# Expert weights of a streaming MoE step: who issues the up blocks

## What is computed

```python
def hier_moe(h, w_r1, b_r1, w_r2, b_r2, w_g, w_u, w_d):
    x = h.reshape(B * S, Dm)
    ...  # routing: top-1 of 4 groups, then top-2 of 8 experts in the group
    for e in range(N_EXPERTS):                 # 32 experts, D_EXPERT = 512
        a = jax.nn.silu(x @ w_g[e]) * (x @ w_u[e])
        y = y + gate[:, e:e + 1] * (a @ w_d[e]).astype(jnp.float32)
    return y.astype(h.dtype).reshape(B, S, Dm)
```

## Time and profile before

| what | us |
|---|---|
| median of three runs | 932.31 |
| the profiled execution | 933.53 |
| its span, first to last instruction | 931.7 |
| PE busy | 776.2 (83%) |
| ACT busy | 116.7 (13%) |
| loads of expert weights, median from issue to landing: down / gate / up | 17.1 / 20.9 / 23.9 |

### The profile page before, as it was taken

One profiled execution on the slowest core, in us unless ns is written; L12 is line 12 of the kernel. 1 busy time (PEld: TensorE's weight loads), 2 busy tenths in 40 slices (PEclk: granted clock), 3 DMA queues, 4 the chain that ended last, 5 costly groups with the idle time before them and its releaser, 6 DMA issues.

```text
span 931.7 us, 11609 instructions
## 1 busy us (share of the span) xinstructions
PE 776.2 (83%) x4652; PEld 463.7 (50%) x4652; DVE 191.4 (21%) x482; ACT 116.7 (13%) x279; POOL 123.9 (13%) x220
## 2 busy tenths in 40 slices
PE   5999999698889999889878797878888788888840
PEld 4756655445654655545544454444545454545420
DVE  2002332225232062411110101010100110101114
ACT  3101311014112042000000000000000000000001
POOL 2100000100001001232111212121111211111123
PEclk9899999989899999789999899999999998999975
DMA  8946952330056434508999999999999999999814
GB/s 247 376 150 225 327 182 91 113 124 1 2 191 253 151 113 160 191 19 340 403 415 422 403 417 414 409 411 387 419 404 421 415 417 416 415 413 418 365 50 129
DMA packets 71599, 261.27 MB, mean 280 GB/s; under 512 B 14055, under 2 KB 30463, under 8 KB 62960
## 3 DMA queue, kind: packets, MB, share of 16 engines
q1 hardware_dynamic: 63232, 244.57, 67.3%
q0 software_dynamic: 8192, 16.27, 5.2%
q10 hardware_dynamic: 144, 0.00, 0.0%
HBM read 249.37 MB, written 24.97 MB: 294 GB/s over the span
## 4 chain that ended last, share of the span: by engine, by line
PE 53%; DMA 34%; DVE 5%; issue 3%; ACT 1%; POOL 1%; SPq 1%; ACTq 0%; POOLq 0%; DVEq 0%
DMA ring<-in_w_exp_gate 32%; PE pA L1048 12%; PE pA L1054 10%; PE pA L1448 10%; PE pS L1468 7%; PE pTr L1041 1%; DMA zone<-y_d,slot 1%; PE pS L1125 1%; PE pS L1104 1%; DVE zone L1853 1%; PE pA L1356 1%; PE pA L1201 1%; PE pA L1071 1%; PE pS L1118 1%; PE pS L1456 1%
## 5 line engine op out<-in xcount | busy, mean ns | idle before, releaser
L1448 PE MATMUL pA<-ring,zone 128*64 128x256 f32 x1984 | 256.3, 417 | 53.4 <-DMA ring<-in_w_exp_gate 53.4
L1448 PEld LDWEIGHTS pA<-ring,zone 128*64 128x64 f32 x1984 | 160.9, 151 | 146.9 <-DMA ring<-in_w_exp_gate 57.2
L1468 PE MATMUL pS<-ring,zone 128*64 128x512 f32 x512 | 117.0, 598 | 21.6 <-DVE zone L1853 21.6
L1048 PE MATMUL pA<-hT,ring 128*128 128x320 f32 x320 | 92.5, 449 | 2.3 <-DVE hT L1541 2.0
L1468 PEld LDWEIGHTS pS<-ring,zone 128*64 128x64 f32 x512 | 37.2, 137 | 80.8 <-issue 77.8
L1048 PEld LDWEIGHTS pA<-hT,ring 128*128 128x128 f32 x320 | 62.4, 198 | 28.0 <-issue 3.1
L968 ACT ACTIVATE zone<-pS 128x512 f32<-128x512 f32 x32 | 19.1, 597 | 370.8 <-PE pS L1468 370.8
L1842 DVE TENSOR_TENSOR zone<-zone,pA 128x256 f32<-128x256 f32 x32 | 13.5, 422 | 252.0 <-ACT zone L961 252.0
L697 POOL COPY idx_cur<-srow 64x1 uint32 (+1 forms) x32 | 5.7, 178 | 336.3 <-PE pTr L1433 334.8
L1853 DVE COPY zone<-pS 128x256 f32<-128x256 f32 x32 | 13.6, 425 | 178.9 <-PE pS L1456 178.9
L1054 PE MATMUL pA<-ring,hT 128*128 128x512 f32 (+1 forms) x112 | 49.9, 604 | 0.0
(11 more groups left out here) (265 smaller groups left out, 648.1 us busy)
## 6 DMA issues: line engine op xcount, KB each, us to landing
ring<-in_w_exp_down SPq DMA_DIRECT2D x32, 2048.0 KB, 17.1
ring<-in_w_exp_up SPq DMA_DIRECT2D x31, 2048.0 KB, 23.9
ring<-in_w_exp_gate SPq DMA_DIRECT2D x31, 2048.0 KB, 20.9
ring<-in_w_in SPq DMA_DIRECT2D x6, 2048.0 KB, 14.3
y_d<-zeros SPq DMA_DIRECT2D x1, 8192.0 KB, 43.7
ring<-in_w_out SPq DMA_DIRECT2D x2, 2048.0 KB, 9.4
ring<-in_w_ck SPq DMA_DIRECT2D x1, 2048.0 KB, 17.2
ring<-in_w_cv SPq DMA_DIRECT2D x1, 2048.0 KB, 21.2
```

What stands on the lines that cost most here:

```text
L1048: last = mm(bank[:, 0:n], w[:, c, m * P:(m + 1) * P], xT[:, c, 0:n], start=c == 0, stop=c == C - 1)
L1448: last = mm(pA[b][half * SLOTS:(half + 1) * SLOTS, x * HF:(x + 1) * HF], xeT[:, b, c, :], w[:, c, half * HF:(half + 1) * HF], start=c == 0 ...
L1468: last = mm(pS[b][half * SLOTS:(half + 1) * SLOTS, 0:512], aT[:, b, f % 2, (f // 2) * SLOTS:(f // 2 + 1) * SLOTS], w[:, f, half * 512:(hal ...
```

## The change

The up blocks of experts 3 to 31 (29 loads) are no longer issued by SP but by ACT, on ACT's own DMA queue; gate and down blocks stay with SP. ACT's stream gets a function `load_up`, called right behind `sigmoid` of the expert that last used the slot: that sigmoid has already waited for `up_read`. The up block of expert 4 is now issued behind the sigmoid of expert 0. The up blocks of experts 0 and 1 and both `ahead` blocks stay where they were. The bytes moved, the slots and PE's, DVE's and POOL's instructions are the same.

```diff
@@ sync
-            def pair(r, p, first=False):
+            def pair(r, p, ups=False):
                 for b in range(2):
-                    for n in range(3):
-                        expert_weights(r, 2 * p + b, b, n, first)
+                    for n in (0, 1, 2) if ups else (0, 2):
+                        expert_weights(r, 2 * p + b, b, n)
...
             expert_weights(0, 2, 0, 2)
-            for n in range(3):
-                expert_weights(0, 3, 1, n)
+            expert_weights(0, 3, 1, 0)
+            expert_weights(0, 3, 1, 2)
             expert_weights(0, 4, 0, 0, before=0)
-            expert_weights(0, 4, 0, 1, before=0)
             expert_weights(0, 4, 0, 2)
-            for n in range(3):
-                expert_weights(0, 5, 1, n)
+            expert_weights(0, 5, 1, 0)
+            expert_weights(0, 5, 1, 2)
@@ scalar
+            def load_up(e, b):
+
+                src = i["w_exp_up"][0, e] if isinstance(e, int) else i["w_exp_up"][0, bass.ds(e, 1)].rearrange("a k n -> (a k) n")
+                act.dma_start(by_k(3 * b + 1), src.rearrange("(p c) n -> p c n", c=C)).then_inc(e_in[3 * b + 1], 16)
...
                 sigmoid(n, 0, first)
+                load_up(4 if first else 2, 0)
                 expert(r, 1, 1, first, first)
+                load_up(3, 1)
                 expert(r, 2, 0, False, first)
+                if not first:
+                    load_up(4, 0)
                 expert(r, 3, 1)
-                with act.Fori(2, NE // 2) as p:
+                load_up(5, 1)
+                with act.Fori(2, NE // 2 - 1) as p:
                     for b in range(2):
                         expert(r, p * 2 + b, b)
+                        load_up(p * 2 + b + 2, b)
+                expert(r, NE - 2, 0)
+                expert(r, NE - 1, 1)
```

More of the change, by code:

```diff
@@ L576, in _ @@
                 with sp.Fori(1, ROUNDS) as r:
-                    with sp.Fori(0, NE // 2) as p:
+                    pair(r, 0, True)
+                    with sp.Fori(1, NE // 2) as p:
                         pair(r, p)
```

## The result

The changed kernel takes **939.39 us** (median; 933.78 to 942.73), the kernel before 932.25 us beside it (928.88 to 935.07). The ratio is 1.0073, with a 95% interval from 1.0055 to 1.0091: slower, clearly, by 0.5 to 0.9%. The ratio is not the quotient of the two medians (939.39 / 932.25 is 1.0077).

A forecast was written before the change was run, and what follows sets the result against it. Full DMA engines, with PE waiting for gate blocks, were taken as the bound. The terms -5.2 + 5.2 + 0.8 + 0.2 + 0 gave +1.0 us on 932.3, so 933.3 us, range 928 to 938.5.

The forecast's parts named there:

- What bounds the kernel: From 446 to 877 us the DMA engines are full, and PE waits once per expert, for its gate block.
- 5.0 us each: Check behind gate 31: up 31 and down 31 land between 877.2 and 887.2 us, supporting about 5.2 us per block.
- Up 4 goes into the idle place: Up 4 fills the idle DMA stretch from 408 to 421 us, so later gates wait for one block less: -5.2 us.
- Up 4 beside the gather: Up 4, issued 0.9 us behind expert 2's gather at 407.38, delays it by +0.8 us, bounds 0 and 4.9.
- The rival of a held-up gather: Expert 2's gather is held up by the full 4.9 us, adding 5.1 in all: 937.4 us, chance 0.1.
- Each later up block overtakes: Up blocks on ACT's queue are served before the next gate, putting every gate one block later: +5.2 us, once.
- Up 3 beside gate 3: Sharing the wires, gate 3 comes late by 2.7 us, and a short idle gap may follow near 450 us: +0.2.
- The rate: Two queues on the same engines leave the rate from 446 to 877 us unchanged: 0, bounds -9.2 and +10.6 us.
- two hardware queues: Rival: alternating between two queues costs DMA rate from 446 to 877 us: +6.3, 938.6 us, chance 0.19.
- The issue on ACT: Issuing 29 up blocks from ACT, behind the sigmoid and ahead of the copy, delays nothing: 0.
- the tail: From gate product 31 to the last down product, PE's and DVE's own work, 19.4 us, stays unchanged.
- the rival of a late issue: ACT reaches up 4's load late, behind a wait, so -5.2 is missing and +5.2 stays: 938.5 us, chance 0.02.

The follow-up runs named there:

- e7: Kernel before, one queue on SP, with every gate from expert 3 on issued behind the same expert's up block; 937.96 us, ratio 1.0070.
- e13: Repeat of e7, the kernel before with each gate issued behind its expert's up block on SP's one queue; 939.81 us, ratio 1.0069.
- e1: Changed kernel, with ACT waiting for expert 2's gather to land before it issues up 4; 935.84 us, ratio 1.0045.
- e2: Changed kernel with up 4 issued at its old time, all up blocks from 3 on still on ACT's queue; 941.56 us, ratio 1.0106.
- e10: The changed kernel itself, repeated beside e11; 941.16 us, ratio 1.0081.
- e11: Repeat of e1, the changed kernel with up 4 issued after expert 2's gather has landed; 937.75 us, ratio 1.0044.
- e12: Repeat of e2, the changed kernel with up 4 at its old time; 941.98 us, ratio 1.0090.
- e6: Kernel before with the gates of experts 3 to 31 on ACT's queue instead of ups, gate 4 at its old time; 928.97 us, ratio 0.9975.
- e3: Kernel before with only up 4 moved to ACT, early behind expert 0's sigmoid, the other blocks on SP's queue; 932.56 us, ratio 0.9988.
- e4: Kernel before with only up 4 moved to ACT, issued after expert 2's gather has landed; 929.32 us, ratio 0.9966.

## Why the prediction was wrong

By its own steps:

- **What bounds the kernel: right, but one check of it was misread.** The DMA share of 446 to 877 us is 1.01 again, and PE waits for gate blocks as before. The check "5.0 us each" behind gate 31 does not hold. The kernel before, from 877 to 888 us:

```profile
877.00:888.00 11.00, 10.13 (x60) 5.12 (x62) 0.42 (x1) 0.60 (x1) 0.00 (x0) 0.84 0.50 206
```

At 206 GB/s, 11 us are 2.3 MB, about one block and not two: when the last part of gate 31 lands, half of what is queued behind it has been moved already, and in these 11 us the DMA engines are idle for half of the time. A landing is told by the last of the 16 engines; the queue is not served block by block. The 5.2 us for a block has better support in the 5.4 us of e7 and e13.
- **Up 4 goes into the idle place (-5.2): right in sign.** -3.9 us on one queue, -5.7 on the own queue (e1 against e2). Two blocks gave 10.5, of which the trace places 7.3 in the stage. This term and the next were to be the same block and to cancel exactly; measured, they are 3.9 to 5.7 and 6.5 to 8.3, and they do not cancel.
- **Up 4 beside the gather (+0.8): the step that failed first.** The prediction placed the issue behind the sigmoid, at 408.3, 0.9 us after the gather's issue. It went out at 405.02, before the sigmoid had begun, 0.4 us ahead of the gather, and the gather paid 5.4 us, more than the upper bound of 4.9. It landed at 413.8, where the prediction had named 411.5 as the sign of being wrong. In the time it is 2 to 3.5 us, by the ratios and the pair e10 and e11. The error was to read an order in ACT's stream as an order in time: the issue has no wait of its own, and the wait for `up_read` ahead of the sigmoid was all that held it. The rival of a held-up gather, at 0.1, named this part of the mechanism; its 937.4 is nearer than the forecast, with the overtaking still too small in it.
- **Each later up block overtakes (+5.2): right in kind, sized too low.** Measured 6.5 to 8.3 us with the own queue (10.0 in e12), 6.0 and 7.8 without one (e7, e13). In the traces one block, 5.4 us, is lost ahead of gate 9, as forecast. What the term left out is 1.2 to 1.8 us in the cycles behind it, and 2.0 to 2.6 us more ahead of gate 9 when the up blocks have their own queue.
- **Up 3 beside gate 3 (+0.2): right place, wrong size.** PE waited 2.90 us at gate 3's product (2.7 was forecast). The idle place near 450, given 0 to 2 us, measured 2.5 us in e1, where the clock fell. In the changed kernel the product took 3.67 us, and the DMA share was 0.87 and 0.92 in the two stretches from 452 to 458 us, 0.6 us of idle time.
- **The rate (0): not settled.** The GB/s of 446 to 877 fell from 413 to 408, below the 411 that the prediction had named as the sign of a lost rate, and it stays at 409 when the stretch is cut at gate product 31. The time for an expert hardly moved, 15.75 us against 15.72. The rival's reason, two hardware queues, does not explain the fall: e7 has it with one queue, and e6, with two, has it not. Its 938.6 is the nearest of all the prices given, and that is luck: it stands for a loss at every expert and has nothing for the gather.
- **The issue on ACT (0), the tail: right.** Gate product 31 to the end of the last down product: 19.4 us in both.
- **The sum and the range.** With the measured terms: the own queue +8.3, the gap -5.7, the gather 2.6 to 3.4, together 5.2 to 6.0, where 7.1 was measured (5.1 to 8.5 by the interval). This is a check of the bookkeeping, not an independent one: the three are differences between the same kernels. The gather's term and the overtaking's were too small in the same direction, and the range was built on the rivals' single prices, not on their sum. Its upper end, 938.5, is inside the measured kernel's interval; the median is 0.9 above it. Two slips of the working changed nothing: the upper bound of the rate is +10.7, not +10.6, and the rival of a late issue, 938.5, keeps the 0.8 for a gather that it would not have met.
- **The Trainium skill.** The rule of "DMA: Bandwidth & Descriptors", section "Issuing engines are not separate DMA queues", that a second issuer saves only issue time, would have given 932.3. No run shows a gain in bandwidth, which agrees with it. But the choice of queue is not neutral: with the same bytes, e2, e6 and the kernel before differ by 11 us (+8.3, -3.0, 0). What the same page's section "Queues, rings and completion order" says, that an engine goes round its queues, is what e6 and the up blocks' 11.7 us agree with.

## What to carry to other kernels

Where the DMA engines are full, ask first how many bytes are served ahead of the block that the busy engine waits for: here a queue of its own for blocks that nothing waited for cost time. Look first for a stretch in which the engines idle because the issuer waits for something else. Filling that stretch from the same queue, one reordering and one wait, was worth 10 us here, where the change lost 7. Before a large load is pulled forward, look for the small transfers on the critical path that it will meet, and hold it back until they have landed.

## What was not expected of the hardware

- A DMA that stands behind an activation in ACT's stream, with no wait between them, was issued while the activation's table was still loading: 405.02 against 406.26 for the activation's start, and the same in e3 and e10 (issue 0.06 us behind the start of the table load each time). The later ones go out 0.01 us behind the start of the activation ahead of them (429.22 against 429.21). A wait between them held it (e1, e4).
- A small transfer (an expert's rows, or the list of 40 KB) that met a block of 2 MB on another queue paid 3.3 to 5.4 us: 8.4, 7.4 and 6.3 us for a gather of 3.0, 6.8 us for a list of 2.1.
- In a second hardware queue beside a full first one, a block of 2 MB landed in 11.7 us, where the `ahead` up block of the changed kernel took 8.0 (a DMA share of 0.69 from 376 to 386 us) and an up block behind the first queue's backlog 24.0.
- The 16 DMA engines do not end a block together. When gate 31 had landed in the kernel before, 2.1 MB of the two blocks behind it, 4.2 MB, were left to move.
